# Two-by-two Strassen blocks for a part of the gate and up projections in all three feed-forward stages, with weight sums made by transfers

## The reference

```python
# stages 0 and 1 (conv_ffn): gate and up are the two halves of one matrix, 22 x 128 columns each
u = causal_dwconv(nrm(x) @ up_w, conv_w, conv_b)      # three taps along the positions
x = x + (silu(u[gate half]) * u[up half]) @ down_w
# stage 2 (swiglu): no convolution
x = x + (silu(nrm(x) @ w_gate) * (nrm(x) @ w_up)) @ w_down
```

## Time and profile before

| what | value |
|---|---|
| three runs, median (lowest to highest) | 2400.45 us (2397.28 to 2402.44) |
| profiled execution, its own time | 2399.27 us |
| its span, first to last instruction | 2397.5 us |
| granted TensorE clock, mean | 0.998 of full speed |
| busy: PE, DVE, ACT, POOL | 99%, 62%, 45%, 15% |
| moved from and to HBM | 94 GB/s over the span |

### The profile page before, as it was taken

The page is one execution under the profiler, slowest core; times in us unless marked ns, Lnnn a source line. Parts: engine busy times, 40 slices in busy tenths (PEclk is TensorE's granted clock), DMA queues, the critical chain, the costliest instruction groups (busy, mean ns, idle before and its releaser), DMA issues.

```text
span 2397.5 us, 30764 instructions
## 1 busy us (share of the span) xinstructions
PE 2371.2 (99%) x11952; PEld 1944.2 (81%) x11952; DVE 1484.8 (62%) x2356; ACT 1086.1 (45%) x1878; POOL 357.9 (15%) x286
## 2 busy tenths in 40 slices
PE   8999999999999999999999999999999999999999
PEld 6677878888888877788888877787788878898987
DVE  6778776763666777766456547534655445873763
ACT  6654554442445677644234334324443334442433
POOL 0252252210111000122011100001210001100001
PEclk9999999999999999999999999999999999999999
DMA  4532223223223221232332332231234332233232
GB/s 164 109 93 79 80 70 99 97 86 108 97 83 120 75 76 49 73 108 92 93 106 87 91 131 84 71 102 57 72 123 136 115 106 79 81 105 99 95 97 89
DMA packets 74847, 226.24 MB, mean 94 GB/s; under 512 B 8144, under 2 KB 12368, under 8 KB 74576
## 3 DMA queue, kind: packets, MB, share of 16 engines
q1 hardware_dynamic: 70272, 215.90, 28.1%
q10 hardware_dynamic: 4432, 8.39, 2.0%
HBM read 215.87 MB, written 8.39 MB: 94 GB/s over the span
## 4 chain that ended last, share of the span: by engine, by line
PE 60%; DVE 1%; ACT 0%; issue 0%; DMA 0%; POOL 0%; POOLq 0%; DVEq 0%; ACTq 0%; SPq 0%
PE bank L1272 59%; PE bank L1276 1%; DVE t L2230 1%; DVE t L2233 1%; ACT t L1715 0%; DVE t L2241 0%; DMA t<-in_w 0%; POOL t L2877 0%; ACT t L1718 0%; ACT L1718 0%; DVE t L2237 0%; DVE t L2798 0%; POOLq L3100 0%; DVEq L3100 0%; DVE t L2644 0%
## 5 line engine op out<-in xcount | busy, mean ns | idle before, releaser
L1272 PE MATMUL bank<-t 128*128 128x512 f32 (+5 forms) x11526 | 2346.4, 369 | 19.1 <-DVE t L2233 7.9
L1272 PEld LDWEIGHTS bank<-t 128*128 128x128 f32 (+2 forms) x11526 | 1901.0, 186 | 433.3 <-issue 80.1
L1715 ACT ACTIVATE t<-t 128x1024 fp32r<-128x1024 f32 (+5 forms) x676 | 564.0, 847 | 564.6 <-PE bank L1272 276.6
L2230 DVE TENSOR_TENSOR t<-t 128x1024 fp32r<-128x1024 f32 (+7 forms) x774 | 687.3, 901 | 202.9 <-ACT t L1715 192.4
L1718 ACT ACTIVATE t<-t 128x512 f32<-128x512 f32 (+6 forms) x610 | 367.5, 616 | 455.8 <-DVE t L2230 307.1
L2877 POOL TENSOR_TENSOR t<-t 128x512 f32<-128x512 f32 (+4 forms) x206 | 316.3, 1542 | 1551.9 <-ACT t L1718 559.7
L2230 DVE TENSOR_TENSOR t<-bank,t 128x512 f32<-128x512 f32 (+4 forms) x434 | 279.2, 648 | 425.2 <-PE bank L1272 414.7
L2233 DVE SCALAR_TENSOR_TENSOR t<-t 128x512 f32<-128x512 f32 (+5 forms) x536 | 386.6, 733 | 102.3 <-ACT t L1718 63.8
L1715 ACT ACTIVATE t<-bank 128x512 f32<-128x512 f32 (+4 forms) x184 | 84.7, 477 | 205.4 <-PE bank L1276 146.9
L2880 POOL TENSOR_SCALAR t<-t 128x128 f32<-128x128 f32 (+3 forms) x64 | 40.9, 645 | 478.6 <-ACT t L1715 247.6
L2233 DVE SCALAR_TENSOR_TENSOR t<-bank,t 128x512 f32<-128x512 f32 x56 | 38.5, 688 | 68.8 <-PE bank L1272 68.8
(11 more groups left out here) (30 smaller groups left out, 53.0 us busy)
## 6 DMA issues: line engine op xcount, KB each, us to landing
t<-in_w SPq DMA_DIRECT2D x304, 512.0 KB, 3.4
t<-in_w SPq DMA_DIRECT2D x48, 384.0 KB, 3.0
t<-in_w SPq DMA_DIRECT2D x56, 320.0 KB, 3.0
t<-in_w SPq DMA_DIRECT2D x28, 256.0 KB, 2.8
tab<-t ACTq DMA_DIRECT2D x1, 2560.0 KB
t<-in_x SPq DMA_DIRECT2D x8, 256.0 KB, 5.0
t<-tab SPq DMA_DIRECT2D x8, 256.0 KB, 3.7
spill<-t ACTq DMA_DIRECT2D x1, 2048.0 KB, 8.3
```

Of the source, the lines that this page charges most:

```text
L1272: return eng.matmul(out, lhs, rhs, start=start, stop=stop, skip_group_check=loose)
L1715: return eng.activation(out, in_, ACT.Copy, scale=scale)
L2230: return eng.tensor_tensor(out, a, b, o)
```

## The change

Quads are used in all three stages: 7 each in stages 0 and 1 (f = 7, 9, 12, 14, 16, 18, 20), 10 in stage 2 (4, 7, 8, 10, 12, 13, 15, 16, 18, 19, where it was 4, 5, 7, 8, 10, 12, 13, 15, 16, 18, 19). The order of the products is new, and so are the units: the first holds one product (p1), the other three two each (p5, p6; p3, p7; p2, p4). The weight sums are no longer made by DVE alone: SP loads 128 x 1536 of weights into one of two sets of sums (19 products ahead, the second set lies in the scratch tiles of the norms), POOL issues a transfer that adds 128 x 1024 from HBM to it (15 ahead) and one that adds 128 x 512 from SBUF (9 ahead), and DVE makes one addition of 128 x 512 after the cut of the second unit (`add3`). The sums of the data's side are made in each stage, in stages 0 and 1 twelve ticks apart. In the quads of stages 0 and 1 the convolution follows, and DVE, not POOL, multiplies gate by up.

```diff
-QUADS = (4, 5, 7, 8, 10, 12, 13, 15, 16, 18, 19)
-PRODUCTS = ("p1", "p2", "p6", "p5", "p7", "p3", "p4")
+QUADS = {0: (7, 9, 12, 14, 16, 18, 20), 1: (7, 9, 12, 14, 16, 18, 20), 2: (4, 7, 8, 10, 12, 13, 15, 16, 18, 19)}
+PRODUCTS = ("p1", "p5", "p6", "p3", "p7", "p2", "p4")
+QUAD_HALF = {"p1": (0, 0), "p5": (1, 0), "p6": (1, 1), "p7": (2, 0), "p3": (2, 1), "p4": (3, 0), "p2": (3, 1)}
...
+    def quad(self, s, f, gate, gate_c, up, up_c):
...
+        region = self.region((gate, 0, 4, gate_c + f * P, P), (up, 0, 4, up_c + f * P, P),
+                             (up, 4, 4, up_c + f * P, P), (gate, 4, 4, gate_c + f * P, P))
+        first = self.load(region, 0, S)
+        last = self.load(region, 2 * S, UNIT)
+        sources = (("raw", first, S), ("s12", (s, f), UNIT), ("s34", (s, f), UNIT), ("raw", last, UNIT))
         for i, product in enumerate(PRODUCTS):
-            if i % 2 == 0:
-                age, self.cut_age = self.cut_age, 1 if i == 4 else self.cut_age
-                u = self.ring(sources[i // 2])
...
+            if QUAD_HALF[product][0] == len(g.units):
+                g.units.append(self.ring(sources[len(g.units)]))
+            self.put(Piece(g, QUAD_HALF[product][0], i, i + 1, i == 0))
...
-        self.start("sum1", f, t - 5)
-        self.start("sum2", f, t - 3)
+        self.start("base", (s, f), t - 19)
+        self.start("add1", (s, f), t - 15)
+        self.start("add2", (s, f), t - 9)
+        self.start("add3", (s, f), max(t - 1, max(at for at, units in self.cut_at.items() if g.units[1] in units)))
...
-        for k in range(4):
-            self.once("tees", k, lambda k=k: self.past("rms", "n2", 3) and (k == 0 or self.past("tees", k - 1, 4)))
+        apart = 4 if s == 2 else 12
+        for k in range(4 if QUADS[s] else 0):
+            self.once("tees", (s, k), lambda k=k: self.past("rms", src, 3) and (
+                k == 0 or self.past("tees", (s, k - 1), apart)))
...
     def quads(T):   # ACT
-        for product, age in (("p1", 1), ("p6", 3), ("p5", 4)):
+        for product, age in (("p1", 1), ("p5", 2), ("p6", 3)):
...
     def quads(T):   # DVE
-        for f in at("sum1", T):
...
-        for f in at("sum2", T):
...
+        for kind, age in (("ga", 8), ("up", 9)):
+            for s, f in at("quad", T - age):
+                if s < 2:
+                    taps((kind, s, f))
...
+        for sf in at("add3", T):   # DVE, after the cuts of the tick
+            w.wait_ge(*K.loaded(last))
+            w.wait_ge(*sig["cut"].at(plan.quad_units[sf][3]))
+            tt(sums[:, 2 * S:3 * S], sums[:, 2 * S:3 * S], buf.raws[last % N_W][:, S:UNIT], ADD).then_inc(*sig["sum"].up(sf))
...
+    def adds(T):   # POOL, ahead of ffn(T)
+        for sf in at("add1", T):
+            w.wait_ge(*K.based(sf))
+            eng.dma_start(K.sums(sf)[:, 0:UNIT], K.region(region)[:, S:3 * S], accum_op=ADD).then_inc(
+                *sig.added[i][0].up())
+        for sf in at("add2", T):
+            w.wait_ge(*K.added(sf, 0))
+            eng.dma_start(K.sums(sf)[:, 2 * S:3 * S], K.sums(sf)[:, 0:S], accum_op=ADD).then_inc(*sig.added[i][1].up())
...
+    def base(sf):   # SP, after the loads of the tick
+        if before:
+            w.wait_ge(*sig["cut"].at(plan.quad_units[before][4]))
...
+        eng.dma_start(K.sums(sf)[:, 0:3 * S], K.region(region)[:, 0:3 * S]).then_inc(*sig.base[i].up())
```

More of the change, by code:

```diff
@@ L293, in feat_steps @@
         self.pending.append(g)
[L295 to L299, removed]
+    def quad(self, s, f, gate, gate_c, up, up_c):
+        key = ("gu", s, f)
+        self.until(lambda: self.past("tees", (s, 3), 6 if f == QUADS[s][0] else 23) and self.place(
+            [((*key, "b"), 0, 10), ((*key, "d"), 1, 6), ((*key, "a"), 5, 4)]), key)
@@ L541, in ffn @@
             for f in range(f0, f0 + nf):
[L542 to L543 removed]
+                if f in QUADS[s]:
+                    self.quad(s, f, gate, gate_c, up, up_c)
                     continue
@@ L1114, in raw_read, with sums_at, sums, based @@
     def raw_read(self, r):
-        users = [u for u, (kind, n, _, _) in enumerate(self.plan.units) if kind == "raw" and n == r]
+        users = [u for u, (kind, n, _) in enumerate(self.plan.units) if kind == "raw" and n == r]
         done = [self.sig["cut"].at(u) for u in users]
-        for f, (first, *_) in self.plan.quad_units.items():
-            if r in (first, first + 1):
-                done.append(self.sig["sum"].at(f, "s2"))
-        return done
+        for sf, (_, last, *_) in self.plan.quad_units.items():
+            if r == last:
+                done.append(self.sig["sum"].at(sf))
+        return done
+    def sums_at(self, sf):
+        n, before = QUADS[sf[0]].index(sf[1]), [q for q in QUAD_LIST[:QUAD_LIST.index(sf)]]
+        turn = 1 + sum(QUADS[s].index(f) % 2 == n % 2 for s, f in before)
+        return n % 2, turn, (sf[0], QUADS[sf[0]][n - 2]) if n >= 2 else None
+    def sums(self, sf):
+        return self.buf.sums[self.sums_at(sf)[0]]
+    def based(self, sf):
+        i, turn, _ = self.sums_at(sf)
+        return self.sig.base[i].at(turn)
+    def added(self, sf, j):
+        i, turn, _ = self.sums_at(sf)
+        return self.sig.added[i][j].at(turn)
     def tee(self, i):
@@ L1936, in quads @@
-        for f in at("quad", T - 7):
-            vg, _ = K.quad_rows(f)
-            w.wait_ge(*sig["q_row"].at(f))
-            func(ACT.Silu, vg[:, :], vg[:, :]).then_inc(*sig["fsilu"].up(2, f))
-        for f in at("quad", T - 9):
-            src, i = h_of(2, f)
-            hi, _ = buf.operand(src, i)
-            w.wait_ge(*K.gated(2, f))
-            if f >= 12:
-                w.wait_ge(*full(("dn", 2, 0, DC - 1)))
-            copy(hi, K.quad_rows(f)[1][:, :], -1.0).then_inc(*sig["hi"].up(src, i))
+                copy(out, K.of(("gu", s, f, QUAD_BANK[product]))[:, 0:H2]).then_inc(*sig["q_copy"].up(s, f, product))
@@ new lines, in quads @@
+        for age in (10, 7):
+            for s, f in at("quad", T - age):
+                if age == (10 if s < 2 else 7):
+                    vg, _ = K.quad_rows(f)
+                    w.wait_ge(*(sig["tap"].at(("ga", s, f), 2) if s < 2 else sig["q_row"].at(s, f)))
+                    func(ACT.Silu, vg[:, :], vg[:, :]).then_inc(*sig["fsilu"].up(s, f))
+        for age in (12, 9):
+            for s, f in at("quad", T - age):
+                if age == (12 if s < 2 else 9):
+                    src, i = h_of(s, f)
+                    hi, _ = buf.operand(src, i)
+                    w.wait_ge(*K.gated(s, f))
+                    if f >= 12:
+                        w.wait_ge(*full(("dn", s, 0, DC - 1)))
+                    copy(hi, K.quad_rows(f)[1][:, :], 1.0 if s < 2 else -1.0).then_inc(*sig["hi"].up(src, i))
@@ new lines, in fu_free, with taps @@
+    def fu_free(n, s):
+        if n >= 3:
+            w.wait_ge(*sig["tap"].at(("ga" if (n - 3) % 2 == 0 else "up", s, (n - 3) // 2), 2))
+    def taps(key):
+        kind, s, f = key
+        n = 2 * f + (kind == "up")
+        ft = f + FFC * (kind == "up")
+        v, ub = buf.fv[n % 6], buf.fu[n % 3]
+        for k in (1, 2):
+            w.wait_ge(*(sig["tap0"].at(key) if k == 1 else sig["tap"].at(key, 1)))
+            stt(v[:, :], ub[:, 2 + k:S + 2 + k], pc(f"fcw{s}", 3 * ft + k), v[:, :], MUL, ADD).then_inc(
+                *sig["tap"].up(key, k))
@@ L3042, in sync_program @@
                 load(plan.units[u][1] + N_W)
+        for sf in at("base", T):
+            base(sf)
         for h in at("tb", T):
```

362 lines of the change are left out of this document (210 added, 152 removed).

## The result

The changed kernel takes **2432.66 us** (median of 4 runs, 2430.38 to 2433.39) where the kernel before took 2398.86 beside it (4 runs): 1.0137 times as long, 95% interval 1.0124 to 1.0150. The forecast was 2408, its range ended at 2426. The direction was right, the size was not: the loss is 34 us, not 8.

A forecast was written before the change was run, and what follows sets the result against it. PE's queue was taken to bound the kernel: 24 quads at 241.9 us plus 21.3 of waits, 263.2 against 255.1, is +8.1 on 2399.3, forecast 2408 us. The range was 2393 to 2426.

The forecast's parts named there:

- 1.17 us late: Stages 0 and 1, quads behind a plain pair: third unit's cut late, p3 starts 1.17 us late; twelve times, 14.0 us.
- "0" at f = 12: Three quads behind the down projection: no taps or gate-and-up product lie ahead, the cut is in time, wait 0.
- 0.62: Stage 2, quads behind another quad: 0.51 us late, then 0.1 late at p3; four times 0.62, 2.5 us.
- 0.96 us late: Stage 2, quads behind a plain pair: third unit's cut late, p3 starts 0.96 us late; five times, 4.8 us.
- I take 1.29 everywhere: Stage 2, POOL's multiplication before a quad: 1.29 us, not 1.68, since DVE's weight sums go; with 1.68 waits total 6.8.
- The rival of late adding transfers: Adding transfers at three times the plain price: 1 us in each of 24 quads, 2432 us; chance 0.09.
- The adding transfers ... I take 0: Base load and adding transfers: 10.7 us, 16.9 with adding ones at twice the price, within 17.8 of lead; cost 0.
- the double price: The two adding transfers at twice a plain transfer's price: three transfers take 16.9 us, still in time.
- Covered, cost 0, but barely: DVE in stages 0 and 1: pair and quad need 19.3 of 20.96 us, so cost 0.
- I take 0: Data's sums in stages 0 and 1: 17.3 us of DVE per stage, pairs leave 23; cost 0, above 3.3.
- The late cut that I followed: Third unit's cut, its first product due at t+3, before at t+4: waits before products sum to 21.3 us.

The follow-up runs named there:

- With POOL's order mended: Changed kernel, POOL's multiplication ahead of the tick's transfers; second adding transfer 7 ahead, not 9, for stage 2 quads behind another: 2423.36 us, ratio 1.0099.
- with the third unit sooner: Changed kernel, third unit split and cut one tick earlier where a quad does not follow another quad: 2409.48 us, ratio 1.0046.
- the kernel with the sooner base load: Changed kernel, base load of quad f = 7 in stages 0 and 1 issued 23 products ahead, not 19: 2429.48 us, ratio 1.0127.
- with the tick: Changed kernel with one empty tick ahead of the attention and one ahead of the mixing stage: 2427.07 us, ratio 1.0121.

## Why the prediction was wrong, point by point

- **"1.17 us late"**, behind plain pairs in stages 0 and 1: right. Ten of the twelve quads wait that long before p3. Quads take 11.33, not 11.25, because the first product behind a wait takes 0.1 more. "0" at f = 12: 10.13.
- **"0.62", stage 2 behind a quad**: right. Forecast were 0.51 before p5 and 0.1 before p3, 10.70 in all; measured 0.46 and 0.11, with 0.07 more in p5 and 0.10 in p3, 10.82 in all.
- **"0.96 us late", stage 2 behind a plain pair**: right only where POOL is free. 11.52 at f = 4 is a wait of 1.35: DVE, still at its cuts, evacuates `up` 0.68 behind the quad's start and not 0.27. With POOL's order mended 7 and 18 wait 0.94 to 0.95, and 10 does so also without it.
- **"I take 1.29 everywhere"**: the step that failed in stage 2. The multiplication itself takes 1.28 to 1.33 where nothing runs beside it, as said. But I costed its duration and not its start. I had written that POOL "stands in its queue while it waits for them", and then priced the transfers' own lateness and not what was queued behind that stand. At 15 and 18 the start is late at the very multiplication that I followed, at 7 at the one before it, 4.2 us; the wait before p3 is 1.4 to 2.4 us above my 0.96 at the three. The rival of late adding transfers had the wrong form too: not 1 us in each of 24 quads, but waits of 2.4 to 3.4 us in four of them.
- **"The adding transfers ... I take 0"**: failed. The sum of 10.7 us, or 16.9 at the double price, against 17.8 of lead held in the median (5.0 + 5.5 + 4.1 = 14.6, plus 0.9 of issue each) and not at their longest: 21.6 us at quad 10, and 7.9 for a base load before quad 18. Medians were compared with a slack of one microsecond. By the estimate from the Trainium skill (DMA: Bandwidth & Descriptors, "Anatomy of one DMA"), 3.2 and 2.6 us, the sum would have been in time everywhere; measured are 5.5 and 4.1.
- **"Covered, cost 0, but barely"**, DVE in stages 0 and 1: right: with the third unit sooner six of stage 0's seven quads take 10.07 to 10.44. **"I take 0"** for the data's sums, above it 3.3 us: the stages lost 3.7 at f = 7, but by POOL's stand for the base load, as the kernel with the sooner base load shows. The 0.665 was itself a mean of two kinds: of the twelve additions of the earlier trace rows, ten take 0.47 to 0.49 us and two take 1.59, with a multiplication of POOL beside them.
- **What is missing altogether** is, first, the attention, +8.6 us. The forecast counted PE's work and waits in the blocks that the diff touches and took the rest of the plan as fixed. The plan is computed; a quad has 7 pieces, and the rule `self.T % 2 == 0` stood in the code to be read. And it is the granted clock: the forecast took 1.00 throughout, and the clock cost 1.5 us in the attention and 4.0 in the quads 15 and 18.
- **The sum.** 8.1 forecast; +4.7 for f = 7 and the slower product behind each wait, +12.1 for stage 2, +8.6 for the attention, and -2.8 of stretches elsewhere give 30.7 of the 31.1 found. The late cut that I followed was forecast at 21.3 us of waits, and taking it away gave 23.2 back, some of that in the stage 2 quads where POOL is late as well. What I did not price is the rest: queues, phase and clock.

## What to carry to other kernels

An asynchronous transfer that waits on the engine that issues it has two prices: its own lateness, and the start of the next instruction in that queue. Write down, for every wait added to a queue, which instruction stands behind it and when its input is ready. Where a planner places work by ticks, compute its output for the changed kernel in all stages, those that the diff does not name too; a changed count of pieces can cost as much as the change is worth. And compare a lead with the transfer's longest time in a busy stretch, not with its median.

## What the runs showed of the hardware

- **An adding transfer occupies the DMA engines about twice as long per byte.** On the page of the changed kernel q0, which carries only the 48 adding transfers, has 4.7% for 18.88 MB and q1 29.5% for 228.48 MB: 0.249 against 0.129% per MB, 1.93 times. At equal packet size it is as much: packets of 4096 bytes take 328 ns in the median in q0 and 159 in q1, those of 2048 bytes 178 and 84. The Trainium skill (Collectives: The Full Stack, "The bandwidth ceiling: the fold count and why AG ≠ RS ≠ AR") says of the add in a collective that it needs two source reads where a copy needs one. The ratio here agrees with that, but no run has a plain transfer in q0, so the queue's own part is not told apart. To issue one holds POOL for 0.87 to 0.89 us in the mean.
- **POOL's multiplication held up a DVE addition for its whole length.** DVE's four additions for the data's sums took 3.65 us where POOL's whole multiplication fell on them (stage 0, from 464.61, changed kernel, beside the POOL row at 466.36 above) and 2.23 in the kernel with the base load sooner, where only its end did. The first three took 0.48 each; the fourth, begun at 465.91, took 2.34 and ended 0.29 after the multiplication, at 468.25. The forecast had them at 0.665 each, 2.7. The other way round, POOL's multiplication took 2.21 where it began 0.17 behind a cut of DVE, and 1.29 beside an idle DVE.
- **The granted clock fell behind two of the long waits.** Windows of the changed kernel within quads 15 and 18:

```profile
2277.42:2285.70 8.28, 6.07 (x50) 5.87 (x49) 3.82 (x4) 3.97 (x7) 2.18 (x2) 1.00 0.21 37
2285.70:2289.20 3.50, 3.50 (x19) 3.50 (x19) 1.23 (x3) 0.72 (x1) 0.00 (x0) 0.51 0.49 150
...
2313.18:2319.80 6.62, 4.47 (x37) 4.26 (x35) 2.33 (x5) 2.22 (x5) 2.18 (x2) 1.00 0.43 78
2319.80:2326.60 6.80, 5.75 (x27) 5.75 (x28) 2.86 (x4) 1.89 (x5) 0.00 (x0) 0.50 0.27 77
```

In both PE had stood for 2 to 3 us, and then 3.5 and 6.8 us ran at a granted clock of 0.51 and 0.50, that is at 1.2 GHz and not 2.4. PE's busy time in these quads rises from 10.33 to 11.82 and 12.86, so 4 of stage 2's 12.1 us are the clock's. In the same execution it did not fall behind the waits of 2.3 and 2.2 us in quads 7 and 10. In others it did at quad 7, behind waits of 2.15 (with the tick) and 2.18 (with the sooner base load), and in the kernel with POOL's order changed at f = 7 of stages 0 and 1, behind 1.80 and 1.83, where the changed kernel waited 1.81 and 1.82 and kept 1.00. So the same wait came with and without the fall, each fall behind a wait in a quad cost some 1.5 to 2.5 us of PE's busy time, and what decides no run here shows.
